# A down-projection whose first feature blocks are split before the last up round, in other PSUM banks

## The reference

```python
def _conv_ffn(h, w_up, conv_w, conv_b, w_down):
    T = h.shape[1]
    u = h @ w_up                                   # 1024 -> 5632
    pad = CONV_W // 2
    up = jnp.pad(u, ((0, 0), (pad, pad), (0, 0)))
    u = sum(up[:, i:i + T] * conv_w[i] for i in range(CONV_W)) + conv_b
    a, gate = jnp.split(u, 2, axis=-1)
    return (jax.nn.silu(gate) * a) @ w_down        # 2816 -> 1024
```

## Time and profile before

| | us |
|---|---|
| median of 3 runs | 1774.73 |
| the 3 runs | 1774.19, 1774.73, 1776.84 |
| the profiled execution | 1774.21 |
| its span, first to last instruction | 1772.4 |
| TensorE matmuls busy | 1693.1 (96%) |
| VectorE busy | 1084.8 (61%) |
| ScalarE busy | 737.6 (42%) |
| mean granted TensorE clock | 0.987 |

### The profile page before, as it was taken

The page is one execution under the profiler, slowest core; times in us unless marked ns, Lnnn a source line. Parts: engine busy times, 40 slices in busy tenths (PEclk is TensorE's granted clock), DMA queues, the critical chain, the costliest instruction groups (busy, mean ns, idle before and its releaser), DMA issues.

```text
span 1772.4 us, 26577 instructions
## 1 busy us (share of the span) xinstructions
PE 1693.1 (96%) x10056; PEld 1519.9 (86%) x10056; DVE 1084.8 (61%) x1949; ACT 737.6 (42%) x1258; POOL 99.1 (6%) x85
## 2 busy tenths in 40 slices
PE   6999999898999999899989999999899999998998
PEld 6788898777999999788868889977799999996886
DVE  4676586566655555576568557874665555546585
ACT  3532135526544444333273323363664444443243
POOL 0021041000000000000000400600000000000000
PEclk9999999999999999999999999999999999999999
DMA  8343165252222222244414415623332222223451
GB/s 320 111 136 120 60 220 160 60 161 77 84 71 77 77 71 72 82 141 146 147 48 131 124 49 179 224 63 103 84 111 71 71 83 71 71 83 101 129 174 60
DMA packets 64734, 196.03 MB, mean 111 GB/s; under 512 B 15248, under 2 KB 16656, under 8 KB 64016
## 3 DMA queue, kind: packets, MB, share of 16 engines
q1 hardware_dynamic: 50224, 176.58, 31.8%
q10 hardware_dynamic: 14432, 18.39, 3.2%
HBM read 188.09 MB, written 6.85 MB: 110 GB/s over the span
## 4 chain that ended last, share of the span: by engine, by line
PE 81%; DVE 7%; ACT 5%; issue 3%; DMA 2%; ACTq 1%; SPq 0%; DVEq 0%
PE bank L1408 12%; PE bank L1409 12%; PE bank L1410 12%; PE bank L1688 12%; PE bank L1684 12%; PE bank L1686 11%; DMA raw<-in_stream 2%; PE bank L1646 2%; DVE ada_sq L911 2%; ACT sp L824 1%; PE bank L1632 1%; DVE w_lo L906 1%; PE bank L1439 1%; PE bank L1573 1%; PE bank L1430 1%
## 5 line engine op out<-in xcount | busy, mean ns | idle before, releaser
L1684 PE MATMUL bank<-aT_hi,w_lo 128*128 128x256 f32 (+1 forms) x1408 | 332.7, 310 | 6.9 <-DVE aT_lo L951 4.4
L1688 PE MATMUL bank<-aT_hi,w_hi 128*128 128x256 f32 (+1 forms) x1408 | 335.4, 313 | 0.0
L1686 PE MATMUL bank<-aT_lo,w_hi 128*128 128x256 f32 (+1 forms) x1408 | 330.0, 307 | 0.0
L561 ACT ACTIVATE w_hi<-raw 128x1024 fp32r<-128x1024 f32 (+1 forms) x120 | 123.2, 1030 | 429.1 <-PE bank L1410 376.7
L906 DVE TENSOR_TENSOR w_lo<-raw,w_hi 128x1024 fp32r<-128x1024 f32 (+1 forms) x120 | 147.1, 1229 | 222.5 <-ACT w_hi L561 222.4
L1684 PEld LDWEIGHTS bank<-aT_hi,w_lo 128*128 128x128 f32 x1408 | 261.5, 191 | 8.2 <-issue 5.2
L1366 DVE SCALAR_TENSOR_TENSOR cv<-bank,par,cv 128x127 f32<-128x127 f32 (+2 forms) x264 | 99.6, 433 | 267.0 <-ACT cv L874 267.0
L1686 PEld LDWEIGHTS bank<-aT_lo,w_hi 128*128 128x128 f32 x1408 | 258.5, 189 | 0.0
L1688 PEld LDWEIGHTS bank<-aT_hi,w_hi 128*128 128x128 f32 x1408 | 255.6, 188 | 0.0
L1408 PE MATMUL bank<-w_hi,aT_lo 128*128 128x512 f32 x560 | 230.3, 411 | 15.0 <-DVE aT_lo L951 8.3
L1409 PE MATMUL bank<-w_lo,aT_hi 128*128 128x512 f32 x560 | 225.4, 402 | 0.0
(11 more groups left out here) (172 smaller groups left out, 2444.7 us busy)
## 6 DMA issues: line engine op xcount, KB each, us to landing
raw<-in_stream SPq DMA_DIRECT2D x320, 512.0 KB, 3.6
bias<-in_bias ACTq DMA_DIRECT2D x8, 896.0 KB, 9.9
na_v<-vn ACTq DMA_DIRECT2D x2, 1280.0 KB, 6.3
x<-in_xs SPq DMA_DIRECT2D x2, 1024.0 KB, 8.7
vt<-na_v ACTq DMA_DIRECT2D x16, 128.0 KB
gb_mix<-gates ACTq DMA_DIRECT2D x2, 1024.0 KB, 4.3
gb_ffn<-gates ACTq DMA_DIRECT2D x2, 1024.0 KB, 7.4
out_ys<-x SPq DMA_DIRECT2D x4, 512.0 KB, 2.6
```

The source lines that it names most:

```text
L561: act.activation(w_hi[:, g % 4, 0:n], raw[:, s % 4, 0:n], ACT.Copy).then_inc(hi_done, 1)
L1684: pe.matmul(out, wl, aT_hi[:, k, tok], start=k == 0, stop=False)
L1686: pe.matmul(out, wh, aT_lo[:, k, tok], start=False, stop=False)
L1688: i_ = pe.matmul(out, wh, aT_hi[:, k, tok], start=False, stop=k == KD - 1)
```

## The change

Blocks 0 and 1 get places of their own, `mx_hi` and `mx_lo`, which share their memory with `y_ffn` (written only after the first half). ScalarE and VectorE leave their loops one round earlier and write the last round out. Ahead of it they split blocks 0 and 1. In its column 3 they split blocks 2 and 3, behind the middle tap on ScalarE and behind the convolution on VectorE, and ahead of the weight granule. Blocks 4 and 5 now wait only for the end of the up-projection (`kt_free`). TensorE's wait for the last convolution moves behind the first down group; in that group each tile waits for the convolution of the column that had its bank. The tiles take banks 0, 4, 1, 5, 2 (`DOWN_BANKS`). Since the next layer's first in-projection block follows in the same banks, the table of banks of the in-projection changes, and the transposes ahead of it use 3, 6, 7 in place of 5, 6, 7.

The diff. Left out are the hunks that only put `DOWN_BANKS[tt]` or `in_bank(0, tt)` in place of `tt` (`tile_squares`, `post_tile`, `first_half`, `first_block`), that of `tp_banks`, and the bodies that moved unchanged into functions:

```diff
@@ -243,6 +243,9 @@
             cv = sb("cv", [P, 4, TOK], F32, s)
             gb_ffn = sb("gb_ffn", [P, 2, D], F32, s)
             sq_ffn = sb("sq_ffn", [P, W], F32, s)
+            with ExitStack() as s2:
+                mx_hi = sb("mx_hi", [P, 2, TOK], F32R, s2)
+                mx_lo = sb("mx_lo", [P, 2, TOK], F32R, s2)
             y_ffn = sb("y_ffn", [P, NT, W], F32, s)
 
@@ -373,8 +376,11 @@
 
         halves = [(DH * (h % 2), h // 2) for h in range(H)]
 
+        IN_BANKS = [(0, 4, 1, 5, 2), (3, 6, 0, 4, 1), (5, 2, 3, 6, 0), (5, 4, 6, 7, 0), (5, 4, 6, 7, 0)]
+        DOWN_BANKS = IN_BANKS[0]
+
         def in_bank(b, tt):
-            return (4, 5, 6, 7, 0)[tt] if b >= 3 else (NT * b + tt) % 7
+            return IN_BANKS[b][tt]
 
         def qk_bank(b, tt):
 
@@ -502,7 +508,7 @@
 
         def kt_free(n, kt, layer):
 
-            if n == 0 and kt < 4:
+            if n == 0 and kt < 6:
                 return at(w_used, layer, W_DOWN0)
             before = kt - 4 if kt >= 4 else max(k for k in range(KF) if k % 4 == kt)
             gi = next(i for i, kts in enumerate(DOWN_KT[n]) if before in kts)
@@ -861,24 +867,46 @@
-                with act.Fori(0, KF // 2) as j:
...
+                def gate_silu(j, c):
+                    act.wait_ge(conv_done, at(conv_done, layer, 4 * j + c + 1))
+                    act.activation(cv[:, c, :], cv[:, c, :], ACT.Silu).then_inc(silu_done, 1)
+
+                def column_mid(j, c):
+                    act.wait_ge(w_used, at(w_used, layer, 4 * j + W_UP0 + c + 1))
+                    act.wait_ge(m_done, at(m_done, layer, 2 * j + c // 2 - 1))
+                    bias_ = par[:, bass.ds(2 * j + (layer * NPAR + C_CB + (c % 2) * KF + c // 2), 1)]
...
+
+                def column_weight(j, c):
+                    act.wait_ge(raw_full[c], at(raw_full[c], layer, 16 * (j + (S_UP0 // 4 + 2))))
+                    act.activation(w_hi[:, c, :], raw[:, c, :], ACT.Copy).then_inc(hi_done, 1)
+
+                def down_high(n, kt, dst):
+                    act.wait_ge(m_done, at(m_done, layer, kt + 1))
+                    act.activation(dst, m[:, kt, :], ACT.Copy).then_inc(mhi_done, 1)
+
+                with act.Fori(0, KF // 2 - 1) as j:
                     for c in range(4):
...
+                        column_mid(j, c)
+                        column_weight(j, c)
                         if c == 2:
-                            gate_silu(1)
-                    gate_silu(3)
+                            gate_silu(j, 1)
+                    gate_silu(j, 3)
+                for kt in range(2):
+                    down_high(0, kt, mx_hi[:, kt, :])
+                for c in range(4):
+                    column_mid(KF // 2 - 1, c)
+                    if c == 3:
+                        for kt in (2, 3):
+                            act.wait_ge(w_used, kt_free(0, kt, layer))
+                            down_high(0, kt, m_hi[:, kt, :])
+                    column_weight(KF // 2 - 1, c)
+                    if c == 2:
+                        gate_silu(KF // 2 - 1, 1)
+                gate_silu(KF // 2 - 1, 3)
                 for gi in range(G_DOWN):
                     if 2 <= gi and gi + 2 < G_DOWN:
                         split_hi(W_DOWN0 + gi + 2, layer)
@@ -886,11 +914,10 @@
                     if gi == G_HALF:
                         half_squares(1, 0, layer)
                     for kt in DOWN_KT[n][i]:
-                        if n and kt >= KT_KEPT:
+                        if n and kt >= KT_KEPT or n == 0 and kt < 4:
                             continue
                         act.wait_ge(w_used, kt_free(n, kt, layer))
-                        act.wait_ge(m_done, at(m_done, layer, kt + 1))
-                        act.activation(m_hi[:, kt % 4, :], m[:, kt, :], ACT.Copy).then_inc(mhi_done, 1)
+                        down_high(n, kt, m_hi[:, kt % 4, :])
@@ -1356,28 +1383,51 @@
-                with dve.Fori(0, KF // 2) as j:
+
+                def column_conv(j, c):
+                    t_ = cv[:, c, :]
+                    dve.wait_ge(tap_mid, at(tap_mid, layer, 4 * j + c + 1))
...
+                    i_.then_inc(conv_done, 1)
+
+                def column_weight(j, c):
+                    dve.wait_ge(hi_done, at(hi_done, layer, 4 * j + (W_UP0 + 4 + c + 1)))
+                    dve.tensor_tensor(w_lo[:, c, :], raw[:, c, :], w_hi[:, c, :].bitcast(F32),
+                                      ALU.subtract).then_inc(raw_free[c], 1)
+
+                def gated(j, s):
+                    dve.wait_ge(silu_done, at(silu_done, layer, 2 * j + s + 1))
+                    dve.tensor_tensor(m[:, bass.ds(2 * j + s, 1), :], cv[:, 2 * s:2 * s + 1, :],
+                                      cv[:, 2 * s + 1:2 * s + 2, :], ALU.mult).then_inc(m_done, 1)
+
+                def down_low(n, kt, dst, hi):
+                    dve.wait_ge(mhi_done, at(mhi_done, layer, KF * n + kt + 1))
+                    dve.tensor_tensor(dst, m[:, kt, :], hi.bitcast(F32), ALU.subtract).then_inc(mlo_done, 1)
+
+                with dve.Fori(0, KF // 2 - 1) as j:
                     for c in range(4):
...
+                        column_conv(j, c)
+                        column_weight(j, c)
                         if c >= 2:
...
+                            gated(j, c - 2)
+                for kt in range(2):
+                    down_low(0, kt, mx_lo[:, kt, :], mx_hi[:, kt, :])
+                for c in range(4):
+                    column_conv(KF // 2 - 1, c)
+                    if c == 3:
+                        for kt in (2, 3):
+                            down_low(0, kt, m_lo[:, kt, :], m_hi[:, kt, :])
+                    column_weight(KF // 2 - 1, c)
+                    if c >= 2:
+                        gated(KF // 2 - 1, c - 2)
                 for gi in range(G_DOWN):
                     if 2 <= gi and gi + 2 < G_DOWN:
                         n, i = divmod(gi + 2, G_HALF)
@@ -1388,12 +1438,9 @@
                     if gi == G_HALF:
                         first_half(1, layer)
                     for kt in DOWN_KT[n][i]:
-                        if n and kt >= KT_KEPT:
+                        if n and kt >= KT_KEPT or n == 0 and kt < 4:
                             continue
-                        q = KF * n + kt
-                        dve.wait_ge(mhi_done, at(mhi_done, layer, q + 1))
-                        dve.tensor_tensor(m_lo[:, kt % 4, :], m[:, kt, :], m_hi[:, kt % 4, :].bitcast(F32),
-                                          ALU.subtract).then_inc(mlo_done, 1)
+                        down_low(n, kt, m_lo[:, kt % 4, :], m_hi[:, kt % 4, :])
@@ -1796,7 +1843,6 @@
                         pe.wait_ge(conv_done, at(conv_done, layer, 4 * j + c - 3))
                         for k in range(KD):
                             up_product(c, (0, 1), k, True)
-                pe.wait_ge(conv_done, at(conv_done, layer, G_UP))
                 for n in range(2):
                     by_tile = 2 * n
 
@@ -1810,9 +1856,9 @@
                     def down_tile(i, tt):
                         kts = DOWN_KT[n][i]
                         for kk, kt in enumerate(kts):
-                            q = kt % 4
                             tok = slice(tt * P, (tt + 1) * P)
-                            i_ = mm3(bank[tt][:], m_hi[:, q, tok], m_lo[:, q, tok],
+                            hi, lo = (mx_hi, mx_lo) if n == 0 and kt < 2 else (m_hi, m_lo)
+                            i_ = mm3(bank[DOWN_BANKS[tt]][:], hi[:, kt % 4, tok], lo[:, kt % 4, tok],
                                      w_hi[:, i % 4, kk * W:(kk + 1) * W], w_lo[:, i % 4, kk * W:(kk + 1) * W],
                                      i == 0 and kk == 0, i == G_HALF - 1 and kk == len(kts) - 1)
                         if tt == NT - 1:
@@ -1823,10 +1869,14 @@
                     for i in range(G_HALF - by_tile):
                         down_ready(i)
                         for tt in range(NT):
+                            if i == 0 and n == 0:
+                                pe.wait_ge(conv_done, at(conv_done, layer, G_UP - 3 + DOWN_BANKS[tt] % 4))
                             if i == 0:
                                 pe.wait_ge(y_copied, at(y_copied, layer, NT * n + (tt + 1)))
                                 pe.wait_ge(y_sq, at(y_sq, layer, NT * n + (NT + tt + 1)))
                             down_tile(i, tt)
+                        if i == 0 and n == 0:
+                            pe.wait_ge(conv_done, at(conv_done, layer, G_UP))
                     for tt in range(NT):
                         for i in range(G_HALF - by_tile, G_HALF):
                             if tt == 0:
```

50 lines of the change are left out of this document (17 added, 33 removed).

## The result

| | before | changed |
|---|---|---|
| median, first measurement | 1774.46 | 1754.48 |
| its four runs | 1773.95 to 1776.84 | 1752.93 to 1757.31 |
| the profiled execution | 1774.21 | 1753.90 |
| its span | 1772.4 | 1752.1 |
| ScalarE busy | 737.6 | 732.5 |

What follows compares the result with a forecast made beforehand. TensorE was taken to bound the kernel, busy 96% of the span, with a 7.4 us pause before each layer's down-projection. Two gains of 8.8 us made 17.6, from 1774.73 to 1757.1 us; range 1755.0 to 1762.0.

Steps and rivals of the forecast that it cites:

- The banks: In-projection and the transposes ahead of it: new bank numbers keep every wait's place and count; taken as nothing.
- The late hand-over: Second or third down group: VectorE's queue waits for a load, TensorE stands 2.1 us a layer; 1761.3 us, 6%.
- a fetch of code behind the loop: End of TensorE's up loop: an instruction fetch costs up to 3.6 us a layer; 1764.3 us, 3%.
- Column 3: First down group: some tile still waits for the last convolution, leaving 6.6 us of gain; 1768.1 us, 3%.
- the slow start: First down group after the pause: matmuls begin at 1.2 GHz, costing 1.36 us more; the same taken for layer 1.
- The clock: TensorE without a pause for some 440 us: the grant falls to 0.5 for a while; slower, 1798 us, 2%.
- The sum: Whole kernel: two layers at 8.8 give 17.6 us, reaching the end whole; forecast 1757.1 us against the median 1774.73.
- How the numbers follow: Whole kernel: forecast has 83%; range 1755.0 to 1762.0 us; faster 95%, within 0.2% 3%, slower 2%.
- The gain of 8.8 us a layer: First down group: starts at 737.51 instead of 744.91, takes 7.02 us; next group at 744.5 instead of 753.29.
- the start 0.16 us earlier: First down matmul: may start up to 0.16 us earlier, as up matmuls issue before the one ahead has ended.
- The low end: Range's lower bound, 1755.0 us: earlier start 0.3, runs' spread 0.5, and as much again for the new median.
- The peeled round at 0: Last up round written out on ScalarE and VectorE: two table loads of 1.28 us fewer on ScalarE, worth 0.

Runs made afterwards that it cites:

- wait_col3: The changed kernel with TensorE's wait for the last convolution put back ahead of the first down group; 1767.5 us, ratio 0.9954 to the kernel before.
- before_twin: The kernel before, unaltered, measured as a control in the second series; 1776.44 us, ratio 1.0000.
- before_3: The kernel before, unaltered, as a control in the fourth series; 1777.40 us, ratio 1.0005.
- banks_only: The kernel before with nothing but the new bank numbers, order and waits as before; 1776.27 us, ratio 1.0000.
- again: The changed kernel, unaltered, measured a second time, in the first series; 1757.15 us, ratio 0.9894 to the kernel before.
- after: The changed kernel as first measured and profiled; median 1754.48 us, ratio 0.9881 to the kernel before.
- after_3: The changed kernel, unaltered, measured a third time, in the fourth series; 1758.68 us, ratio 0.9902 to the kernel before.
- old_banks: The changed kernel with the old bank numbers, so the fourth tile waits for column 3; 1755.28 us, ratio 0.9880 to the kernel before.

## Why the prediction was right, and where it was wrong

**What held.** The mechanism, step by step. The two pauses were the wait for block 1's low part behind the whole last round. Without them TensorE goes on 0.3 us behind the last pair of up matmuls; the first group takes 7.02 us as worked out. The early splits fit in the idle time ahead of the round. Blocks 2 and 3 had 1.9 us to spare (forecast 1.6), the third group 2.1 (forecast 1.5). The banks are worth nothing elsewhere. The gain reached the end whole: the rest of both down-projections takes as long as before in the traces. VectorE works without a gap from 737.92 to 749.57, and TensorE's busy time fell by 2.2 us (forecast 2.7).

**The rivals.** The late hand-over did not come; nor did a fetch of code behind the loop: 0.30 us lie between the last up pair and the first down matmul, in both layers. The Trainium skill (Runtime: NRT & Kernel Launch, "Instruction fetch mechanics") says that the sequencer fetches the next instructions while it executes the current ones; the trace agrees. Column 3 is not waited for. "wait_col3" is that rival made real. Its price was a gain of 6.6 us (a start 3.3 us earlier, the slow start kept); its segments are 4.0 and 3.8 us shorter than the averages below, and its time is 9.2 us under the kernel before of its series. The 1768.1 us forecast lies beside the 1767.5 measured only because the base was low as well (error 2). That a rest of a pause keeps the whole slow start was right. The clock did not fall: 1.00 in every stretch around the place.

**Where it was wrong: "The sum" and "How the numbers follow".** The mechanism held and its sizes were off. Three errors: two sit in the sum and nearly cancel, the third put the result outside the range.

1. *The gain of 8.8 us a layer.* Its term for the slow start (1.36 us a layer) came from one profiled execution, and that has the shortest slow start of all traces with the full pause. Four traces with the old loops (the first one, "before_twin", "before_3", "banks_only") have segments of 16.12, 16.66, 16.71 and 16.59 in layer 0 and 16.12, 16.29, 16.22 and 16.38 in layer 1, on average 16.52 and 16.25. Their first groups take 8.77 and 8.51 us on average, so the slow start is 1.75 and 1.49 us, 0.5 us more in the two layers than forecast. "I take the same for layer 1" was also unfounded: the slow spell differs from pause to pause. Another 0.3 us is the start 0.16 us earlier, which the prediction saw and put into the range, not into the sum: the first down matmul comes 7.56 us earlier behind the last pair of up matmuls (7.86 - 0.30), not 7.40. With 7.20 in the changed kernel the segments give 9.3 + 9.05 = 18.4 us, against 17.6 forecast.
2. *The anchor.* The 17.6 were taken from 1774.73, the median of three runs. 114 runs of that kernel give 1776.4, with a standard deviation of 2.0. The forecast 1757.1 lies beside the changed kernel's mean, 1756.7, by two errors that nearly cancel, which is luck: the base 1.7 too low, the gain 2.1 too small.
3. *The low end.* The prediction allowed 0.5 us for the spread, from the distance of the median to the lowest of three runs, and 0.5 for the new median. With the earlier start's 0.3 that makes 1.3 us and a low end of 1755.8; why it says 1755.0 it doesn't tell. Single executions of the kernel before go from 1771.5 to 1781.0. Medians of three and of four executions drawn from the 114 have standard errors of 1.4 and 1.1 us. With these in place of 0.5 and 0.5 the low end is 1754.3, and the range holds this result. The first four runs of the changed kernel have a median 2.2 us under its mean of twelve, and the medians of its two other series lie inside the range as stated. Error 1 put right moves the range down by 0.8 us, error 2 moves it up by 1.7. So what the range failed on is the spread of executions, allowed for too narrowly, and no part of the mechanism.

*The peeled round at 0* is a fourth step that runs contradict: -1.7 us with a standard error of 0.35. A part of it is explained, the pause shorter by 0.4 us in each layer. In the changed kernel it is not an extra gain through the pause, which is gone there anyhow.

**What the first two traces say, and what they don't.** The changed kernel's profiled execution is 20.3 us shorter than that of before. Matmul by matmul, 2.95 us of it are there within the first 55 us, where both kernels do the same. TensorE before, in its start:

```profile
37.19 3.58 PE L1439 MATMUL bank<-cond_T,raw 128*128 128x2 f32 x16 [2.11 <-DMA raw<-in_stream]
...
48.66 0.80 PE L1408 MATMUL bank<-w_hi,aT_lo 128*128 128x512 f32 x1 [3.31 <-DVE aT_lo L951]
...
54.38 0.60 PE L1409 MATMUL bank<-w_lo,aT_hi 128*128 128x512 f32 x1
```

and in the changed kernel:

```profile
32.02 7.12 PE L1486 MATMUL bank<-cond_T,raw 128*128 128x2 f32 x32 [0.18 <-DMA raw<-in_stream]
...
47.03 0.80 PE L1455 MATMUL bank<-w_hi,aT_lo 128*128 128x512 f32 x1 [3.31 <-DVE aT_lo L978]
...
50.18 0.43 PE L1456 MATMUL bank<-w_lo,aT_hi 128*128 128x512 f32 x1
```

The first loads land sooner in this execution, and the clock rises after seven slow matmuls of 128x512 instead of fourteen (the last of them starts at 54.38; in the changed kernel the one at 50.18 is the first at the higher level). "again", the same kernel as this one, reaches the same matmul 2.3 us later. The two places of the change account for 8.9 + 8.9 us between these two traces, and the rest is such drift with either sign.

**What stays open.** Of the 19.7 us measured, the segments explain 18.4. The remaining 1.3 has a standard error of about 0.65. The traces give no cause in the change for it: the spans of the four traces with the old loops and of four with the new order ("after", "again", "after_3", "old_banks") are 19.8 us apart on average, 18.4 of it in the two segments and 1.0 in the first 57 us, where the kernels do the same and where traces of one and the same kernel differ by up to 2.3 us. Chance is enough for it, but that isn't shown. The written-out round has a similar remainder: 1.7 measured, 0.7 explained by the segments of its three traces (16.08, 15.97 and 15.93 in layer 0, 16.11, 16.27 and 15.97 in layer 1). It may be the same thing, but no run tells.

## What to carry to other kernels

When an engine that sets the time pauses behind another engine's queue, look for the item in that queue which it really needs, and when that item's inputs were ready: here ten rounds earlier, and moving two blocks' splits ahead and dropping a wait for work that the first group doesn't need was worth 1.1% of the kernel. The pause of 7.4 us costs TensorE more than its length here, by 1.4 to 1.9 us, and half the pause still costs 1.6 to 1.65: the partial fix ("wait_col3") got less than its share, the last few us gave more. Take a price that rests on a clock spell from several traces or state it as a range, and anchor a forecast of 1% on more than three runs.
